# One decoder layer in one kernel: gate A's two chunks of the input projection move, and the attention output's projection is made in three passes

## What is computed

```python
z = h @ w_in                       # h: 576 x 1024; q, k, v of 3 groups | u, v | gA | gB
ga = sigmoid(z[..., gA columns])   # 1024 columns, in two chunks of 512
o_a = dilated attention, 3 groups of 8 heads, groups combined by softmax weight
      # prompt: within the 512 tokens; samples: against caches of keys and values
pa = o_a @ w_pa                    # 576 x 512 times 512 x 1024
pb = o_b @ w_pb
x = x + gate1 * ((ga * pa + sigmoid(gB) * pb) @ w_o)
x = x + gate2 * HierMoE(norm(x))   # 16 experts, 2 per token
```

## Time and profile before

| | |
|---|---|
| median of 3 runs | 1283.09 us (1280.27 to 1287.53) |
| the profiled execution's own time | 1284.33 us |
| its span | 1282.5 us |
| PE busy in the span | 1218.6 us, 95% |
| DVE busy | 665.0 us, 52% |
| ACT busy | 539.6 us, 42% |
| HBM | 234 GB/s over the span |

### The profile page before, as it was taken

One profiled execution on the slowest core, in us unless ns is written; L12 is line 12 of the kernel. 1 busy time (PEld: TensorE's weight loads), 2 busy tenths in 40 slices (PEclk: granted clock), 3 DMA queues, 4 the chain that ended last, 5 costly groups with the idle time before them and its releaser, 6 DMA issues.

```text
span 1282.5 us, 17812 instructions
## 1 busy us (share of the span) xinstructions
PE 1218.6 (95%) x7090; PEld 927.5 (72%) x7090; DVE 665.0 (52%) x925; ACT 539.6 (42%) x856; POOL 198.2 (15%) x229
## 2 busy tenths in 40 slices
PE   4999999999999999998899999999999999999996
PEld 2677877777777887897766756657677888777762
DVE  2428613222161314123577651255678888888877
ACT  4533313102173125316333342121547777778742
POOL 2112200020000010002200020000153222223230
PEclk9999999999999999999799999999979999999999
DMA  9652212264543453547799995730589999999972
GB/s 339 241 214 96 78 66 66 66 213 159 184 154 117 144 205 146 175 177 284 242 349 383 379 335 185 247 107 33 179 266 346 382 373 378 374 374 375 369 279 88
DMA packets 128779, 293.96 MB, mean 229 GB/s; under 512 B 10000, under 2 KB 10128, under 8 KB 124936
## 3 DMA queue, kind: packets, MB, share of 16 engines
q1 hardware_dynamic: 111112, 243.57, 54.2%
q0 software_dynamic: 17600, 49.44, 10.9%
HBM read 269.91 MB, written 30.42 MB: 234 GB/s over the span
## 4 chain that ended last, share of the span: by engine, by line
PE 80%; DMA 9%; ACT 4%; DVE 4%; issue 2%; POOL 1%; ACTq 0%; DVEq 0%; SPq 0%; POOLq 0%
PE psum L1035 18%; PE psum L1036 17%; PE psum L1037 17%; DMA arena<-in_cache_kv_w_dram 5%; PE psum L1023 5%; PE psum L1097 5%; DMA arena<-in_w_up_dram 2%; PE psum L1266 2%; PE psum L1432 2%; PE psum L1339 2%; PE psum L1050 1%; POOL slots_d L953 1%; ACT arena L1648 1%; PE psum L1244 1%; DVE part L2484 1%
## 5 line engine op out<-in xcount | busy, mean ns | idle before, releaser
L1035 PE MATMUL psum<-part,part 128*128 128x512 f32 (+1 forms) x1088 | 437.3, 402 | 6.4 <-DVE part L2524 2.3
L1036 PE MATMUL psum<-part,part 128*128 128x512 f32 (+1 forms) x1088 | 428.0, 393 | 0.0
L1037 PE MATMUL psum<-part,part 128*128 128x512 f32 (+1 forms) x1088 | 427.8, 393 | 0.0
L1035 PEld LDWEIGHTS psum<-part,part 128*128 128x128 f32 (+1 forms) x1088 | 218.9, 201 | 65.7 <-issue 15.4
L1037 PEld LDWEIGHTS psum<-part,part 128*128 128x128 f32 (+1 forms) x1088 | 219.0, 201 | 42.3
L1036 PEld LDWEIGHTS psum<-part,part 128*128 128x128 f32 (+1 forms) x1088 | 219.4, 202 | 38.0
L2484 DVE TENSOR_TENSOR part<-arena,part 128x2048 fp32r<-128x2048 f32 x96 | 217.6, 2289 | 33.9 <-ACT part L1883 32.7
L1883 ACT ACTIVATE part<-arena 128x2048 fp32r<-128x2048 f32 x94 | 178.6, 1919 | 44.2 <-DMA arena<-in_w_up_dram 24.9
L1648 ACT ACTIVATE arena<-psum 128x512 f32<-128x512 f32 (+4 forms) x127 | 73.3, 598 | 266.5 <-PE psum L1037 217.6
L1982 DVE TENSOR_TENSOR part<-arena,part 128x2048 fp32r<-128x2048 f32 x42 | 96.0, 2298 | 155.8 <-PE psum L1097 133.3
L1023 PE MATMUL psum<-cst,arena 128*128 128x128 f32 (+2 forms) x778 | 107.1, 282 | 30.3 <-DMA cst<-in_consts_dram 9.7
(11 more groups left out here) (301 smaller groups left out, 1096.5 us busy)
## 6 DMA issues: line engine op xcount, KB each, us to landing
arena<-in_w_in_dram SPq DMA_DIRECT2D x34, 1024.0 KB, 5.4
arena<-in_cache_kv_w_dram SPq DMA_DIRECT2D x16, 2048.0 KB, 12.3
arena<-in_w_gate_dram SPq DMA_DIRECT2D x32, 1024.0 KB, 9.5
arena<-in_w_up_dram SPq DMA_DIRECT2D x32, 1024.0 KB, 8.6
arena<-in_w_down_dram SPq DMA_DIRECT2D x32, 1024.0 KB, 10.1
arena<-in_w_ada_dram SPq DMA_DIRECT2D x8, 2048.0 KB, 8.4
arena<-in_cache_kv_w_dram SPq DMA_DIRECT2D x16, 1024.0 KB, 10.4
arena<-in_w_ada_dram SPq DMA_DIRECT2D x8, 1024.0 KB, 14.1
```

The source lines that it names most:

```text
L1035: nc.tensor.matmul(out_, hi, w_hi, start=start, stop=False)
L1036: nc.tensor.matmul(out_, hi, w_lo, start=False, stop=False)
L1037: last_product[0] = nc.tensor.matmul(out_, lo, w_hi, start=False, stop=stop)
```

## The change

Gate A's first chunk is projected in group 2's attention, where groups 0 and 1 project the next q chunk; its second chunk takes the first's place at b = 8; after `gather_heads(7)` the kernel goes straight to pa. `w_pa` comes as two halves of 1 MB that are split in hi and lo. The combined prompt result is turned into hi by ACT and lo by DVE, so the `tp` banks of o0 to o3 are emptied by DVE (`turn_lo`), a step of b later. The samples' part has hi from ACT and lo from DVE (`oT4_hi`, `oT4_lo`). The turning of the shift rows moves from before c = 0 to c = 1, and their copy on DVE behind the five tiles of c = 0. Gate results have other places in SBUF; the experts' slots and two scratch tiles are renumbered, since the stream is one entry longer.

```diff
+        AFTER = ("q1", "q2", "ga0")
...
-                if i == 5 and g < 2:
-                    mm.stage(f"q{g + 1}", TILES, "act")
+                if i == 5:
+                    mm.stage(AFTER[g], TILES, "act")
...
             if b == NB:
-                mm.stage("ga0", TILES, "act")
+                mm.stage("ga1", TILES, "act")
...
             if 2 <= b <= 5:
-                tp.stage(f"o{b - 2}", 1, "act")
-        mm.stage("ga1", TILES, "act")
+                tp.stage(f"o{b - 2}", 1, "dve")
         mm.stage("pa", 2 * TILES, "dve")
...
             put_ada(g + 1, 2, 2)
+        put_chunks("ga0", projected("ga0"), w_in, [QKV // CH + 4])
...
             if b == NB:
-                put_chunks("ga0", projected("ga0"), w_in, [QKV // CH + 4])
+                put_chunks("ga1", projected("ga1"), w_in, [QKV // CH + 5])
             if b:
                 kv_slots(b - 1, 1, [mm.first[f"so{b - 1}"]] * 2)
-        put_chunks("ga1", projected("ga1"), w_in, [QKV // CH + 5])
-        put("pa", [mm.first["pa"] + 9], t["w_pa"][0].rearrange("(j p) n -> p j n", p=P))
+        for c in range(2):
+            put("pa", [bank_of("pa", c, 4)], t["w_pa"][0].rearrange("(j p) n -> p j n", p=P)[:, :, c * CH:(c + 1) * CH])
+            split[-1] = True
...
# SP
-                    if n == S0[f"ada{G}"][-1] + SLOTS + 1:
+                    if n == S0[f"ada{G}"][-1] + (SLOTS if G == 3 else SLOTS + 1):
                         store_rows(sp, G)
...
# PE, prompt attention
-                if g < 2:
-                    samples_product(f"q{g + 1}", 0, h4_raw, 0)
+                samples_product(AFTER[g], 0, h4_raw, 0)
                 tile_values(*tiles[2])
-                if g < 2:
-                    project(f"q{g + 1}", H_PARTS, 0, g=g + 1, ahead=((f"q{g + 1}", 0, h4_raw), None))
+                project(AFTER[g], H_PARTS, 0, ahead=((AFTER[g], 0, h4_raw), None))
                 tile_values(*tiles[3])
...
# PE, end of the samples' attention
                 if b == NB:
-                    samples_product("ga0", 0, h4_raw, 1)
-                    project("ga0", H_PARTS, 0)
+                    samples_product("ga1", 0, h4_raw, 1)
+                    project("ga1", H_PARTS, 0)
                     turn_exponentials(NB - 1)
                 if 1 <= b <= NB:
                     attend(b - 1)
-                if b == NB:
-                    for half in range(2):
-                        samples_product("ga1", 0, h4_raw, half)
...
-            project("ga1", H_PARTS, 0)
-            slot_wait(S0["pa"][0])
-            tp.wait_emptied(pe, tp.first[f"ot{NB - 1}"])
-            wpa = slot(S0["pa"][0]).rearrange("p (j n) -> p j n", j=4)
-            pe.wait_ge(shift_in, 32)
-            transposes(tp.first["shift"], 0, 9, [shift9[:, k * P:(k + 1) * P] for k in range(KD)])
+            tp.wait_emptied(pe, tp.first["o3"])
             for c in range(2):
                 if c == 1:
+                    pe.wait_ge(shift_in, 32)
+                    transposes(tp.first["shift"], 0, 9, [shift9[:, k * P:(k + 1) * P] for k in range(KD)])
                     u = tp.first["shift"] + 1
                     pe.wait_ge(rt_in, 16 * 7)
                     tp.wait_emptied(pe, u - 1)
...
+                half_wait(S0["pa"][c])
+                _, wpa_hi, wpa_lo = half_slot(S0["pa"][c])
+                for i in range(4):
+                    m = bank_of("pa", c, i)
                     mm.wait_empty(pe, m)
                     for j in range(4):
...
+                        three_passes(mm.bank(m), wpa_hi[:, j, w], wpa_lo[:, j, w], oT[:, :, o], oT_lo[:, :, o], j == 0, j == 3)
+                    tally(mm_filled)
+                m = bank_of("pa", c, 4)
+                mm.wait_empty(pe, m)
+                pe.wait_ge(o4_lo, 1)
+                for j in range(4):
+                    three_passes(mm.bank(m)[0:NS, :], oT4_hi[:, j, :], oT4_lo[:, j, :], wpa_hi[:, j, :], wpa_lo[:, j, :], j == 0, j == 3)
+                tally(mm_filled)
...
# ACT, after group 2's exponentials and turned tiles
+            act.wait_ge(row_out, 32 * 12)
+            sigmoid_a(0)
...
                 if b == NB:
-                    split_to(S0["ga0"][1])
-                    sigmoid_a(0)
+                    split_to(S0["ga1"][1])
+                    sigmoid_a(1)
+                    split_to(S0["pa"][0])
...
+            nc.scalar.activation(oT4_hi, oT4, ACT.Copy).then_inc(o4_hi, 1)
+            split_to(S0["pa"][1])
             split_to(S0["wo"][1])
...
# DVE, samples' attention and pa
+                if 3 <= b <= 6:
+                    turn_lo(tp.first[f"o{b - 3}"], 0, P, *(x[:, b - 3, :].rearrange("p (k n) -> p k n", k=4) for x in (oT, oT_lo)))
...
                 if b == NB:
                     place_exponentials(NB - 1)
+                    split_to(S0["pa"][0])
...
-            split_to(S0["wo"][1])
+            dve.wait_ge(o4_hi, 1)
+            V.tensor_tensor(oT4_lo, oT4, oT4_hi, ALU.subtract).then_inc(o4_lo, 1)
+            split_to(S0["pa"][1])
+            dve.wait_ge(mix_back, 32)
...
+            for i in range(TILES):
+                mixed(0, i)                     # L2347 and L2349 of before
+                if i == 1:
+                    split_to(S0["wo"][0])
             u = tp.first["shift"]
             tp.wait_filled(dve, u)
             V.tensor_copy(shiftT, tp.bank(u)[:, 0:9 * KD].rearrange("p (k n) -> p k n", k=KD)).then_inc(tp_dve, 1)
-            dve.wait_ge(mix_back, 32)
+            split_to(S0["wo"][1])
+            tp.wait_filled(dve, u + 1)
+            V.tensor_tensor(shift_lg9, tp.bank(u + 1)[0:9, 0:20], brt[0:9, :], ALU.add).then_inc(tp_dve, 1)
+            for i in range(TILES):
+                mixed(1, i)
+                if i == 0:
+                    mix_low(0)
             mix_low(1)
```

More of the change, by code:

```diff
@@ L331, in build @@
         oin = at(MIX0 + 12960, 4, 3 * OW)
+        oin_parts = part(MIX0 + 12960, 4, 3 * OW)
+        oT, oT_lo = (oin_parts[:, :, OW + n * AW:OW + (n + 1) * AW] for n in range(2))
         pnew = at(MIX0 + 19296, 3 * NT)
         gain = at(WK0 + 6144, D)
-        sga = at(WK0 + 7168, TILES, D)
-        sgac = at(WK0 + 7168, KD, SEQ)
-        x1 = sga
+        x1 = at(WK0 + 7168, TILES, D)
+        sgac = at(KEPT0 + 3072, 4, SEQ), oin[:, :, 0:SEQ]
+        sga4 = at(MIX0 + 19504, CH), at(MIX0 + 12288, CH)
         mixP = [parts(HT0 + half * SLOT, HT0 + half * SLOT + HALF, 4, SEQ) for half in range(2)]
@@ L389, in build, with expert_place @@
         xgT, xgT_lo = parts(KEPT0, KEPT0 + 2 * D, 2, KD, P)
+        def expert_place(n):
+            return (n + 1) % SLOTS if n < SLOTS else n
         def expert_half(n):
-            first = n * SLOT
+            first = expert_place(n) * SLOT
             return at(first, 4, CH), *parts(first + HALF, first, 4, CH)
         LAST_BANKS = ((0, 1), (2, 3), (4, 7), (5, 6), (0, 1))
-        yg = at(0, TILES, 2, D)
-        spread = at(TILES * 2 * D, 3, TILES, P)
-        junk_end = at(3 * SLOT, D)
+        yg = at(SLOT, TILES, 2, D)
+        spread = at(SLOT + TILES * 2 * D, 3, TILES, P)
+        junk_end = at(0, D)
         zeros = at(KEPT0 + D, D)
@@ L577, in paired @@
         def paired(name, j):
-            return name != "wo" and (name, j) not in (("v", 0), ("gb", 0))
+            return name not in ("wo", "pa") and (name, j) not in (("v", 0), ("gb", 0))
         def columns_first(name):
@@ L762, in _ @@
             for at_ in range(3):
-                last = max(n for n in range(N_SLOTS) if n % SLOTS == at_)
+                last = max(n for n in range(N_SLOTS) if n % SLOTS == expert_place(at_))
                 wait_slot_read(sp, last)
@@ L1393, in _ @@
                 if b == NB:
-                    samples_product("ga0", 0, h4_raw, 0)
+                    samples_product("ga1", 0, h4_raw, 0)
                 if b >= NB:
@@ L1705, in empty_tiles @@
                     if i == 4 and paired(name, j):
-                        empty_samples(bank_of(name, j, 4), dst[0:NS, 4, cols], func, scale)
+                        empty_samples(bank_of(name, j, 4), dst[0:NS, 4, cols] if cols is not None else dst[0:NS, :], func, scale)
+                    elif cols is None:
+                        empty(mm, bank_of(name, j, i), turned[:, i, :], P, func, scale)
                     elif turned is not None and i < 4:
```

87 lines of the change are left out of this document (32 added, 55 removed).

## The result

The changed kernel takes **1295.12 us** (median of 6 runs, 1289.88 to 1302.98) against 1284.33 for the kernel before in the same comparison (6 runs, 1280.27 to 1287.53): ratio 1.0089, 95% interval 1.0066 to 1.0112. Forecast were 1285.5 us, a range of 1276.0 to 1293.0 and no change. It is slower by more than the 0.5% that a measurement can tell, and outside the range.

The account below looks back on a forecast made before the run. TensorE, busy 95% of the span, was taken to bound the kernel. Terms summed to +2.45 us, giving 1285.5 us against the median of 1283.1, range 1276.0 to 1293.0, forecast as no change.

Parts of the forecast that it names:

- Part 1: Group 2's attention: taking in ga0 costs the difference between groups 1 and 2, 48.3 - 27.4 = +20.9 us.
- into idle time. I cost both at nothing: Group 2: moved key-half loads and SP's eight earlier row stores were both priced at zero.
- a group 2 of over 53 us: Sign of a rival: splits delay exponentials, ACT and DVE set group 2's pace; +25.5 for 20.9, 1290.1 us, chance 0.06.
- The bank behind the sigmoid: Group 2's last value product waits for ACT's table load and two reads to empty its PSUM bank: +2.05 us.
- The samples' opening: Start of the stage after group 2: opens faster if the clock stays full, -1.0 us, ends 0 and -3.2.
- DVE's low parts: Samples' attention: DVE instead of ACT empties a turned tile's bank four times, +0.3 us, ends 0 and 2.2.
- Part 3: End of samples' attention: ga1's matmuls there taken out, -25.5 us; DVE's masking of attend(7) no longer hidden, +0.9.
- Part 4: pa: two chunks in three passes -4.2 us, a new wait +7.3, low clock behind it +1.7.
- The wait for the mix: pa before c = 1: shift rows' copy queues behind five gate products needing the mix, +7.3 us, ends 1.5 and 10.
- The clock behind it: pa after that new wait: one stretch of TensorE at about half clock, +1.7 us, ends 0 and 6.8.
- The slower rival: c = 1 of pa: clock stays low after the wait, 6.8 in place of 1.7, 1290.6 us, chance 0.18.
- I carry the sum to the end: Everything after pa: order kept and loads no later, so the sum of +2.45 us reaches the end unchanged.

Follow-up runs that it names:

- e2: Changed kernel with DVE's split of ga0's first half moved ahead of its wait for the oscr write: 1291.11 us, ratio 1.0060.
- e1: Changed kernel with SP's eight row stores put back one stream entry later: 1293.23 us, ratio 1.0075.
- e6: e5 with pa back in plain fp32, without splits and DVE's low parts: 1284.80 us, ratio 1.0013.
- e5: Changed kernel with the three edits of e2, e3 and e4 together: 1280.85 us, ratio 0.9981.
- e7: e5 with DVE's scratch clearing and shift-logit copies ahead of the low part of the mix's second half: 1276.45 us, ratio 0.9948.
- a1: The changed kernel itself measured again, beside others on one chip: 1296.26 us, ratio 1.0104.
- e3: Changed kernel with the shift rows' transposes and DVE's copy back ahead of pa's first chunk: 1289.73 us, ratio 1.0039.
- e4: Changed kernel with ACT's table load and ga0's samples' sigmoids ahead of group 2's last turned exponentials: 1293.87 us, ratio 1.0065.

## Why the prediction was wrong

**Part 1, the step that failed: "Group 2 gets what group 1 has", +20.9.** The matmuls and splits are the same, but the neighbours in the queues aren't. In group 2 the change also puts eight row stores just ahead of the write to `oscr`, and the split of ga0's first half stands on DVE behind the wait for that write. I had written of the stores "into idle time. I cost both at nothing", and named as their cover the values and key turns, not what else was waiting for a landing in that stretch. They cost 3.98 us of idle and 2.0 of half clock: the term was +26.9. e2 takes out 5.6 of the 6.0 with the split's place alone, e1 shows that the stores made the write late. The twin was not one in before's trace either: DVE waited 2.83 us for this landing in group 2 and not at all in group 1. (The samples' matmuls of a chunk are 32 in group 1, two lots of 16, not the 16 of the prediction; the difference of the groups holds them all.) The chance I had given to a group 2 of over 53 us was 0.06, by another mechanism (splits pushing the exponentials back); no run shows that one.

**The bank behind the sigmoid, +2.05: right.** 2.82 - 0.80 = 2.02 us. The rows read 640.83 for the load and 642.12 for the first sigmoid:

```profile
...
640.83 1.28 ACT L1647 ACT_TABLE_LOAD   x1
642.12 0.77 ACT L1647 ACTIVATE arena<-psum 64x256 f32<-64x256 f32 x2
```

The load is followed 1.29 us after its start by the sigmoid. The Trainium skill's page "ScalarE: Activation LUTs" (section "What ACT_TABLE_LOAD costs") adds a drain of about 1.38 us; this second place doesn't show one either.

**The samples' opening, -1.0, and DVE's low parts, +0.3: together -0.7 forecast, +0.3 measured.** From group 2's last values to the gate chunk it took 150.4 us before and 150.7 after. The opening gave less than forecast: the scores behind DVE's 3.15 us copy began 9.05 us after the last value product before (625.03) and 8.7 after (653.91), where the copy still stood in the way and TensorE waited 1.4 us for DVE just ahead of them:

```profile
...
650.11 3.15 DVE L165 COPY arena<-arena 128x32 f32<-128x32 f32 x1
...
653.91 1.13 PE L1346 MATMUL psum<-arena 128*32 128x136 f32 x32
```

TensorE waited 4 times for the low parts, 2.2 us in all, my upper end; by e6's gather about 1.0 of it reached the end of the stage (e5's and e7's gathers, alike up to there, are 0.8 us apart, so this is rough). The clock wasn't full there, as I had assumed: two stretches of 3.4 us at half clock, from 644.5 and 665.0, followed the waits. From the last value product to attend(7)'s end it took 179.0 us against 178.7, where a longer stretch had been named as a sign of being wrong.

**Part 3, -25.5 and +0.9: right.** attend(7)'s end to pa's start took 27.1 us before and 1.7 after, -25.4, of which 0.6 is the turning of the shift rows, which stands in pa now; the mask's wait is 0.81 us.

**Part 4.** Three passes: -4.2 forecast, -3.4 measured (14.1 instead of 13.7 us a chunk: the matmuls start 0.232 us apart, not 0.228). The wait for the mix: +7.3 forecast, **6.96** (7.1 in a1). VectorE's timeline after, against the earlier trace rows, shows the queue that I had drawn:

```profile
...
838.43 0.69 DVE L2348 TENSOR_TENSOR arena<-psum,arena 128x512 f32<-128x512 f32 x1 [7.58 <-DMA arena<-mixd]
...
841.09 2.28 DVE L1987 TENSOR_TENSOR part<-arena,part 128x2048 fp32r<-128x2048 f32 x1
...
847.27 0.22 DVE L2357 COPY arena<-psum 128x72 f32<-128x72 f32 x1
```

The clock behind it: +1.7 forecast, 2.1 lost (the shift rows' product 0.13 us longer, ten matmuls 0.20 each). The slower rival, a long stretch, half came: its length in the record was 10.2 us, past the mark of 10 that the prediction named for it, but half lay in the idle time. The Trainium skill's page "TensorE: Matmul & The Clock Gate" (section "HAM oscillation — how this bites in real kernels") has matmuls that resume after a long wait pay again at half rate; both waits of 4 and 7 us agree, and the 2.82 us one also had a slow start (2.27 for 1.97 us).

**"I carry the sum to the end": nearly.** The w_o stage to the first token product gave 1.9 us back: the 3.4 us at half clock at 859.8 isn't there after, and the 13.6 us from 931.4 became 3.4 and 6.8. A wait of 2.0 us for the gathered tokens took some of that place. The last token products then came 4.3 us later still; whether by chance or by the new placement the runs above leave open.

By the sum: 2.45 forecast; +6.3 in group 2, +1.0 in the samples' attention, -0.2 behind it and +1.0 in pa (its pace 0.8) make 10.6 at the w_o stage. The medians say 10.8. The mechanism of the change's own parts was right; what was wrong is one thing costed at nothing. By the sum it alone took the result out of "no change": without its 6.3 us the change would stand at +4.3, 0.3%. The runs don't settle that much: e2, without the wait, measured 1.0060 [1.0039, 1.0081], or 7.4 us: inside the range of times, not clearly inside 0.5%. By the sum 3 us of these 7.4 are not accounted for.

## What to carry to other kernels

When a piece of work is moved into a stretch, list for every engine that takes part what *waits* stand in its queue ahead of the piece, and for each such wait what else the change puts in front of the transfer it waits for; a twin stage prices the work, not the queue. An instruction whose inputs are there (a split, a copy of small rows) belongs ahead of a wait on a DMA, not behind it: two such moves, and the sigmoids' ahead of the last turned copies, turned 1.0104 into 0.9981 on one chip. Look, too, for what the moved piece makes wait in turn, as e1, e3 and e4 each showed. And measure the mended change beside the same mend on the old kernel: here over half of the lead was that of an edit which both kernels could have had.

## What was not expected of the hardware

- A write of a tile to DRAM by GpSimd (264 KB, issued near 600 us) released its waiter after 3.7 us in e1, 5.6 us in the kernel before, both without SP's row stores about, and 8.9 us (8.4 in e2) with those eight stores (four of 2 and four of 128 KB, 520 KB together) issued in the 5 us ahead, on another engine's queue. In stretches of 1 us the DMA share first reads under 0.1 from 603 in e1 (release 603.70), from 606 in before (605.90) and from 608 in the changed kernel (609.10), where it had fallen slowly from 0.57 at 603: each time the write let DVE go at about the end of the other traffic. The Trainium skill's page "DMA: Bandwidth & Descriptors" (section "Queues, rings and completion order") has a transfer's completion on a DMA engine land only after every earlier write from that engine, across its queues. The times agree; no run here shows the mechanism itself.
- The lower clock is counted in the idle time too. Of 10.2 us at 1.2 GHz only the 5.1 us that TensorE worked cost anything, and of the 6.8 us from 610.4 only the last 4.0. The mean granted clock loosely follows a kernel's time from run to run: the changed kernel's runs had 0.985 at 1289.9 us and 0.977 at 1303.0, though also 0.986 at 1295.0. e5 and e7, with the three waits gone, have 0.984 to 0.991.
